# Four more weight remainders by accumulating DMA, modulations in a scratch of their own, squares added in pairs, and three changed orders of work

## The reference

```python
x = first_block(x, c, w_ada, ...)                      # 256 x 1024, fp32 throughout
# even layer, for x and for the context
sh, sc, gt = _modulation(c, e_w_mod[i], e_b_mod[i])    # silu(c) @ w_mod + b_mod
x_new = x + gt * _even_mix(_pre(x, e_norm[i], sh, sc), *args)
xc = xc + gt_c * _even_mix(_pre(xc, e_norm[i], sh_c, sc_c), *args)
# _even_mix: u = silu(layernorm(dwconv(a_val * sigmoid(a_glu))))
#            y_a = (u @ a_pw_w + a_pw_b) * silu(a_gate)
#            y_b = fourier_mix(b_val) * silu(b_gate);  concat(y_a, y_b) @ w_out
# odd layer: modulations of its own, rms norms of x and xc, ODD_IN projection, window attention
# _pre(x, g, shift, scale) = rmsnorm(x, g) * (1 + scale) + shift
```

## Time and profile before

| | |
|---|---|
| median of three runs | 747.08 us (745.29 to 749.2) |
| profiled execution | 744.48 us, span 742.7 us |
| PE busy | 725.7 us, 98% of the span |
| DVE busy | 640.5 us, 86% |
| ACT busy | 393.1 us, 53% |
| POOL busy | 8.3 us, 1% |
| chain of work that ended last | PE 79%, DVE 9%, DMA 5%, ACT 3%, issue 2% |
| mean granted TensorE clock | 0.994 of full speed |
| L940 (subtractions) | 82, 2288 ns each |
| L415 (casts) | 90, 1906 ns each |
| L905 (modulation halves) | 88 + 48, 1220 ns each |

### The profile page before, as it was taken

How to read it: one execution, slowest core, us unless ns; L and a number is a source line. 1 busy time by engine, 2 the same in 40 slices (tenths; PEclk the granted TensorE clock), 3 DMA queues, 4 the chain that set the end, 5 groups by cost and what they waited for, 6 DMA issues and landing times.

```text
span 742.7 us, 12665 instructions
## 1 busy us (share of the span) xinstructions
PE 725.7 (98%) x5202; PEld 665.2 (90%) x5202; DVE 640.5 (86%) x1082; ACT 393.1 (53%) x532; POOL 8.3 (1%) x18
## 2 busy tenths in 40 slices
PE   8899999999999999999999999999989999999996
PEld 4789989999989999999999998888768899999995
DVE  5777898897998899999988999999899979888653
ACT  4254366668356555554557555345462345555742
POOL 0000000000000000000000000000000000000000
PEclk9999999999999999999999999999999999999998
DMA  9989999866664676666656176877405642675101
GB/s 367 420 323 395 388 395 355 315 245 216 220 227 170 221 255 253 236 227 235 248 199 227 57 248 157 219 206 192 113 23 227 226 144 83 221 275 187 58 1 57
DMA packets 24875, 163.98 MB, mean 221 GB/s; under 512 B 2758, under 2 KB 4591, under 8 KB 5360
## 3 DMA queue, kind: packets, MB, share of 16 engines
q1 hardware_dynamic: 21404, 150.37, 54.2%
q0 software_dynamic: 1152, 8.39, 5.6%
q10 hardware_dynamic: 2262, 4.42, 1.8%
HBM read 153.71 MB, written 1.07 MB: 208 GB/s over the span
## 4 chain that ended last, share of the span: by engine, by line
PE 79%; DVE 9%; DMA 5%; ACT 3%; issue 2%; DVEq 0%; ACTq 0%; SPq 0%
PE psum L1607 67%; DVE w_lo L905 4%; DMA raw<-in_w 4%; PE psum L1698 3%; DVE w_lo L940 2%; DMA arena<-in_w 2%; ACT w_hi L415 1%; PE psum L2102 1%; PE psum L2126 1%; PE psum L2114 1%; PE psum L1789 1%; PE psum L1646 1%; PE psum L1771 1%; PE psum L1675 1%; DVE xs L1415 0%
## 5 line engine op out<-in xcount | busy, mean ns | idle before, releaser
L1607 PE MATMUL psum<-h_hi,w_hi 128*128 128x256 f32 (+1 forms) x1280 | 386.3, 302 | 3.5 <-DVE h_lo L1381 2.2
L1607 PE MATMUL psum<-h_lo,w_hi 128*128 128x256 f32 (+1 forms) x1280 | 382.6, 299 | 0.0
L1607 PE MATMUL psum<-h_hi,w_lo 128*128 128x256 f32 (+1 forms) x1280 | 382.5, 299 | 0.0
L1607 PEld LDWEIGHTS psum<-h_hi,w_hi 128*128 128x128 f32 x1280 | 244.6, 191 | 13.8 <-issue 4.1
L1607 PEld LDWEIGHTS psum<-h_lo,w_hi 128*128 128x128 f32 x1280 | 244.7, 191 | 7.9 <-issue 0.2
L1607 PEld LDWEIGHTS psum<-h_hi,w_lo 128*128 128x128 f32 x1280 | 244.6, 191 | 7.5
L940 DVE TENSOR_TENSOR w_lo<-raw,w_hi 128x2048 fp32r<-128x2048 f32 x82 | 187.6, 2288 | 26.1 <-ACT w_hi L415 25.2
L415 ACT CAST w_hi<-raw 128x2048 fp32r<-128x2048 f32 x90 | 171.3, 1906 | 38.9 <-DMA raw<-in_w 29.8
L905 DVE SCALAR_TENSOR_TENSOR w_lo<-raw,cond 128x1024 fp32r<-128x1024 f32 x88 | 104.2, 1220 | 0.8
L905 DVE SCALAR_TENSOR_TENSOR w_lo<-raw,arena 128x1024 fp32r<-128x1024 f32 x48 | 56.8, 1220 | 11.4 <-DMA raw<-in_w 5.8
L638 ACT ACTIVATE arena<-psum,vec 128x256 f32<-128x256 f32 x44 | 22.5, 564 | 58.6 <-DVE g_lo L1182 54.2
(11 more groups left out here) (246 smaller groups left out, 710.0 us busy)
## 6 DMA issues: line engine op xcount, KB each, us to landing
raw<-in_w SPq DMA_DIRECT2D x138, 1024.0 KB, 4.9
w_lo<-raw POOLq DMA_DIRECT2D x8, 1024.0 KB, 7.2
arena<-in_w SPq DMA_DIRECT2D x3, 1024.0 KB, 14.6
xs<-in_xs SPq DMA_DIRECT2D x1, 1024.0 KB, 9.0
consts<-diff ACTq DMA_DIRECT2D x4, 256.0 KB, 9.2
cond<-diff ACTq DMA_DIRECT2D x1, 1024.0 KB, 8.6
xs<-in_xs ACTq DMA_DIRECT2D x1, 1024.0 KB, 7.5
out<-xs SPq DMA_DIRECT2D x2, 384.0 KB, 2.5
```

The costliest lines, as they stand in the source:

```text
L1607: last = mm(out, w[a], x[b], start=start and n == 0, stop=stop and n == 2, skip_group_check=skip)
```

## The change

- `BY_DMA` takes in chunks 73 to 76 as well: twelve chunks instead of eight get their low half by negation on ACT and an adding DMA.
- The modulations 39 to 43 (`MODS_APART`) write their products into `arena[:, 8448:9472]` (free there) instead of a `w_lo` slot. They no longer wait for that slot; since all four products go to one place, each waits for the one before.
- In `split` on DVE the modulations before a chunk are done even where the chunk itself goes by DMA. m39 is done in one piece, behind the splits of the Fourier tiles.
- ACT's `load_ln_exp` stands behind the four squares instead of before them.
- Fourier tiles 2 and 3 are gated in the loop that scales and splits `u`, at `t` = 3 and 5.
- Squares of the main tokens' tiles 0 to 5 are added in pairs on DVE (`add_squares_of`), one pair after chunk 73's evacuation, one after chunk 74's, and one after the bias and the coefficients; PE sums three tiles instead of six and waits for all three pairs before. The semaphore of the context's pairs is shared (now 6).
- In `staggered` PE also waits for the remainder of the first chunk.
- On PE, at `h` = 1, `stick_scores(0)` comes before `transposed_probs(0)`.

```diff
-BY_DMA = tuple(range(LIN_EIN + 4, LIN_EIN + 12))
+BY_DMA = tuple(range(LIN_EIN + 4, LIN_OIN + 1))
+MODS_APART = range(39, 44)
@@ scalar, after the even input chunks
-            load_ln_exp()
             for t in range(4):
                 act.wait_ge(sem("centered"), t + 1)
                 nc.scalar.activation(ln_tmp[:, t, :], conv[:, t, :], ACT.Square).then_inc(sem("ln_squares"), 1)
                 if t < 2:
                     fourier_evac(t + 2)
+            load_ln_exp()
             act.wait_ge(sem("ln_sum"), 2)
@@ vector, mod
-                if not isinstance(j, int) or j >= SPL + AS_LOADED:
+                apart = m in MODS_APART
+                products = arena[:, 8448:8448 + D] if apart else None
+                if not apart and j >= SPL + AS_LOADED:
                     dve.wait_ge(sem("lin_done"), LIN_OPEN + j - (SPL - 1))
...
                     for t in range(2):
+                        if apart and (t or v):
+                            if t:
+                                me.mark(last)
+                            me.wait()
                         last = nc.vector.scalar_tensor_tensor(
-                            w_lo[:, slot, D * t:D * (t + 1)], raw[:, rslot, D * t:D * (t + 1)], 1.0, c, ALU.mult, ALU.mult,
+                            products if apart else w_lo[:, slot, D * t:D * (t + 1)], raw[:, rslot, D * t:D * (t + 1)], 1.0, c, ALU.mult, ALU.mult,
                             accum_out=modv[:, bass.ds(4 * m + 2 * t + v, 1)])
@@ vector, split
-                    if j in BY_DMA:
-                        return
                 if isinstance(j, int):
                     for mod_before in mods_before(j)[done:]:
                         mod_static(mod_before, j)
                     mod_before = (mods_before(j) or [None])[-1]
+                    if j in BY_DMA:
+                        return
@@ vector, even layer
-                if t == 1:
-                    fourier_gated(1)
+                if t in (1, 3, 5):
+                    fourier_gated((t + 1) // 2)
 
             (m,) = mods_before(LIN_EOUT + 1)
-            mod_static(m, LIN_EOUT + 1, part=0)
...
-                    if t >= 2:
-                        fourier_gated(t)
...
-            mod_static(m, LIN_EOUT + 1, part=1)
+            mod_static(m, LIN_EOUT + 1)
             split(LIN_PW + 2, done=1)
...
+            def add_squares_of(name, k):
+
+                tiles = gain_sq if name == "odd_ctx" else norm_tmp
+                dve.wait_ge(sem(f"sq_{name}"), k + 2)
+                nc.vector.tensor_tensor(tiles[:, k, :], tiles[:, k, :], tiles[:, k + 1, :], ALU.add).then_inc(sem("odd_added"), 1)
...
+                if i in (1, 2):
+                    add_squares_of("odd_x", 2 * i - 2)
                 if i == 2:
-                    split(LIN_OIN, done=2)
                     mod_bias(36, 44)
                     coefficients(32, "o_norm", mod_row(O_SC, 0))
                     coefficients(40, "o_norm", mod_row(O_SC, 1))
+                    add_squares_of("odd_x", 4)
@@ tensor, staggered
+                if j in BY_DMA:
+                    remainder_ready(j)
                 remainder_ready(j + 1)
@@ tensor, first block, odd h
-                    transposed_probs(p)
                     if p:
+                        transposed_probs(p)
                         weighted_values(p - 1, 1)
                     stick_scores(p)
+                    if p == 0:
+                        transposed_probs(p)
@@ tensor, even output, after the first half of chunk 75
-                        sum_squares("odd_x", range(6))
+                        pe.wait_ge(sem("odd_added"), 3)
+                        sum_squares("odd_x", (0, 2, 4))
                     if s == 1 and m == 0:
                         sum_squares("odd_x", (6, 7))
-                        pe.wait_ge(sem("odd_ctx_added"), 3)
+                        pe.wait_ge(sem("odd_added"), 6)
                         sum_squares("odd_ctx", (0, 2, 4))
```

More of the change, by code:

```diff
@@ L1440, in _ @@
             for k in (0, 2, 4):
-                dve.wait_ge(sem("sq_odd_ctx"), k + 2)
-                nc.vector.tensor_tensor(gain_sq[:, k, :], gain_sq[:, k, :], gain_sq[:, k + 1, :],
-                                        ALU.add).then_inc(sem("odd_ctx_added"), 1)
+                add_squares_of("odd_ctx", k)
             split(LIN_OIN + 1)
```

## The result

| | before | after |
|---|---|---|
| median | 745.16 us (20 runs) | 747.98 us (20 runs) |
| ratio, 95% interval | | 1.0028 (1.0017 to 1.0040), +2.1 us |
| profiled execution, span | 744.48, 742.7 us | 749.54, 747.4 us |
| mean granted clock over the runs | 0.996 (the runs of before in the experiments) | 0.992 |

The forecast was −1.1 us; the kernel became 2.1 us slower (1.3 to 3.0); this is by the ratio, which is estimated from all runs, while the two medians lie 2.8 us apart. It stays inside the 0.5% that counts as no change, and inside the range, but on the other side of zero.

A forecast was written before the change was run, and what follows sets the result against it. PE, busy 98% of the span, was taken as the bound, so only its breaks and removed PE work could be won. −0.77 − 0.35 = −1.1 us gave 743.4 profiled, median 746.0, range 743.0 to 749.0.

The forecast's parts named there:

- what covers the rest: Check that low halves of chunks 73 to 76 and the load for modulation 41 arrive in time; cost taken as 0.
- the added transfers come late: Rival: transfers take three times 7.2 us, PE stands 9.5 us for chunk 75; 755.5 us; chance 0.05.
- the clock falls in the new wait: Rival: PE's 2.8 us idle before the sums lowers the clock, costing 1.7 us of matmul; 747.7 us; chance 0.15.
- the forecast wait: PE's wait for the third addition of squares before its three sums, some 2.8 us, ending at 590.1 us.
- steps 2 to 4: Table load, Fourier tiles and modulation 39, and added DMAs with pairs: together 0.35 us won at the sums.
- step 1: Stick-breaking scores ahead of the first transposed probabilities on PE at h = 1; gain 0.77 us, bounds 0 and 1.1.
- the rival (0.18): Weight loads swallow the gain of the reordered scores at h = 1; only −0.35, 746.7 us; chance 0.18.
- Step 2: ACT's table load at 528.33 moved behind the squares; gain 0.49 us, bounds 0 and 0.5.
- Step 3: Fourier tiles 2 and 3 gated earlier, first half of modulation 39 later on DVE; gain 0.27 us, bounds 0 and 0.3.
- Step 4, DVE's walk: DVE followed from modulation 39 at 555.9 to the third addition's end at 590.05; PE goes on at 590.1.
- Step 4, pairs of squares: Squares added in pairs on DVE, 0.36 us each; three sums less save PE 1.3 us, but it waits for all additions.

The follow-up runs named there:

- experiment 9: Changed kernel with the adding transfer of chunk 74 cut to 16 of its 2048 columns; 746.54 us, 1.0002 to the kernel before.
- experiment 10: Changed kernel with the adding transfers of chunks 74 and 75 both cut to 16 columns; 747.03 us, 1.0009 to the kernel before.
- experiment 6: Changed kernel with 14 matmuls of zeros on PE ahead of its wait for chunk 75; 747.23 us, 1.0024 to the kernel before.
- experiment 12: Kernel of experiment 9 with 12 matmuls of zeros where PE waits for the third addition of squares; 745.56 us, 0.9995 to the kernel before.
- experiment 8: Kernel before with only the stick-breaking scores put ahead of the transposes at h = 1; 745.63 us, 0.9998.
- experiment 11: Kernel of experiment 5 with the old order of scores and transposes at h = 1; 743.00 us, 0.9961 to the kernel before.
- experiment 2: Kernel before with scores ahead, table load behind the squares and Fourier tiles gated earlier, modulation 39 not moved; 744.06 us, 0.9982.
- experiment 3: Changed kernel with the first half of modulation 39 back at its old place; 749.55 us, 1.0048 to the kernel before.
- experiment 5: Kernel of experiment 2 with chunk 73 alone added by DMA, modulation 39 apart at its old places, no main-token pairs; 743.45 us, 0.9970 to the kernel before.
- experiment 7: Changed kernel without the pairs of main-token squares, so PE sums six tiles; 748.27 us, 1.0040 to the kernel before.
- experiment 1: Changed kernel with the old order at h = 1, transposes before stick-breaking scores; 748.92 us, 1.0043 to the kernel before.
- experiment 4: Changed kernel with chunk 74 subtracted on DVE again instead of by DMA; 748.84 us, 1.0043 to the kernel before.

## Why the prediction was wrong

**The step that failed** is in "what covers the rest". It took the slowing of loads beside a transfer at 0 (bounds 0 to 2.5 us), on the grounds that DVE had 0.8 us to spare, and it followed only the load for modulation 41. Take 2.0 us off the times of the profile after, since PE was that much behind the forecast when it came to the last pointwise tile (555.65 against 554.42 − 0.76): then modulation 39 began at 555.9 and SP's load went out at 561.0, both as walked. The load took 9.7 us, just under the "twice" of the upper bound, and DVE waited 2.95 us. Two things were not carried on. The load of chunk 75 goes out 0.4 us behind it and is the third transfer beside the other two: 11.8 us where the walk had counted 4.9, so the negation ended at 577 instead of 572. And the transfer behind it, again beside loads, took 10.8 instead of 7.2. The low half stood ready at 588.1 instead of 579.2, for a need at 584.2: 5.0 us of cover were there and 8.9 were used up, 3.9 us too many; PE came 0.35 us later than walked and waited 3.6. All three signs that the prediction had named for being wrong came: DVE waited for the load before 41, a new transfer landed above 9 us, and the sums started without a wait. All of this was in reach before the run: the walk itself had a transfer and two loads of 1 MB each under way between 561 and 567, and took for each a duration from rows in which it ran alone. The Trainium skill ("DMA: Bandwidth & Descriptors", section "Rules for kernel authors") says of two transfers to disjoint partition halves that they use the same 16 engines and gain nothing over one; the trace agrees for a transfer and two loads: by the shares of the profile after (worked out in the last section) they need 5.2 + 2 × 2.8 = 10.8 us of all 16 engines, and from the first issue to the last landing 13.0 us passed (562.29 to 575.26), with a third load coming in at 568.3 and a fourth at 572.5.

**Rival "the added transfers come late"** had the right place and the right sign with 0.05. It was priced at three times the duration and argued away by the earlier trace rows. But those rows show transfers that run mostly alone. In the trace of before the transfers of the even input are issued at 496.9, 507.8 and 518.6 us, and the loads at 504.0 and 515.0, each just when the transfer ahead of it has landed (7.1 and 7.2 us), since SP waits for it; a load then overlaps the next transfer by 1 us. Where the overlap was longer, 3.5 us at 464.3, the transfer took 8.5. (The longest of those rows, 9.2 us at 453.4, had 0.8 us of a load beside it and stays unexplained.) In the stretch of the change SP has modulation chunks in its order, whose loads wait for DVE and not for the transfer, and so the two come together. The argument was about DVE and never asked what else was moving. DVE's work does not tell the short transfers from the long ones: in before, those at 496.9 and 518.6 us took 7.0 to 7.1 with DVE busy 6.9 of 7.0 us, and in the changed kernel DVE is busy 71% of the time under the transfer of 73 (7.0 us) and under that of 74 (10.2 us) alike; those of 74 to 76 took 10 us and more wherever loads ran beside them. The Trainium skill's rule ("SBUF — State Buffer", section "SBUF: two separate sides"), which the prediction set against the change, doesn't reach this case as the page has it: a DVE operation starves the descriptors while it runs in a 2-port mode, and one with two SBUF inputs, as a modulation or a subtraction is, gets in the way only of a GpSimd operation that reads SBUF. The trace agrees, with 7.0 us under such operations back to back. No run took DVE's modulations away, so a share of it in the longer ones is not excluded.

**Rival "the clock falls in the new wait"** (0.15) came true beside it: in the changed kernel behind the wait for chunk 75, and in experiments 9 and 10 behind the very wait that it named. It was priced well: 1.7 us of matmul at the lower level, against 2.4 us on the 24 short matmuls in the profile after. In the timed runs the mean granted clock fell from 0.996 to 0.992, which is 746 × 0.004 = 3 us of full-speed work not done. Not all of that shows in the time: over the 20 runs of the changed kernel the time rises by 0.56 us (standard error 0.13) for each such microsecond. That makes 1.7 us, an estimate from scatter, while experiments 6 and 12 kept the clock up in one place and won 0.3 and 0.5 by the middles, with overlapping intervals. The two parts can't be added neatly, since in experiment 6 the late addition took over where the clock had been.

**Sum by the runs.** The error is 3.2 us, from −1.1 to +2.1. The collision of the transfer of 74 with the loads is 1.9 of it (experiment 9: +2.1 to +0.15). Of the other 1.3 the clock behind the forecast wait is 0.5 by experiment 12 (+0.15 to −0.4); the last 0.7 is smaller than the intervals, which are 1 us to either side, and is left open.

**The same from marks in the traces.** PE has a 0.16 us wait for a square at 215.3 us and another at 735.5 (times of before), in every trace. Between these two lie 520.15 us in before, 524.35 in the changed kernel, 522.44 in experiment 9 and 519.62 in experiment 12, where the transfer of 74 is out and the clock up: −0.5 us, against −0.35 forecast for steps 2 to 4. So these steps were priced rightly but for the collision and the clock. The 2.8 us between experiments 9 and 12 are what a clock down for 6.8 us cost in one profiled execution; the timed runs of the two differ by 0.5 only, and their mean clocks by less than the two profiles' do. Ahead of the first mark the change has step 1 alone. PE reaches it between 213.9 and 216.2 us, on the average at 215.2 in the 11 traces with step 1 and at 215.7 in the three without, a difference smaller than the spread: the open 0.7 us may be step 1's.

**Step by step.**
- Step 1: right in the trace, its gain not shown. The bracket at the first transposes is gone (but for experiment 8, with its late load) and, in five of the traces, one of 0.2 to 0.4 us stands at the second; yet experiments 8 and 11 find no gain. They speak for the rival (0.18), by which the weight loads set the pace in this stretch, but within intervals that hold the forecast 0.77 too. DVE's normalisation began anywhere between 100.9 and 103.4 us in the traces, and PE's lead of 0.8 us is small against that.
- Step 2: right in the mechanism, and worth more than its upper bound. The table load stands at 532.67 behind the fourth square, none before the first, and PE has no idle time before the sum behind it. From the mark at 215.3 us to the first matmul behind the stop at 541, PE takes 325.35 us in the two traces without this step and 324.6 to 324.7 in the twelve with it: 0.7 us, where 0.49 was forecast and 0.5 was the bound. It is the most exact figure of the study; where the last 0.2 come from was not looked into.
- Step 3: right for both halves together. The wait for the last pointwise low half is 0.3 us instead of 0.56. Where the first half of modulation 39 kept its place (experiments 2, 3, 5 and 11) the wait was 0.7 to 0.8 instead: in experiment 2, which moves the Fourier tiles alone, the step loses a little.
- Step 4, DVE's walk: right where the loads were in time. In experiment 9 the third addition ran from 590.27 and PE went on at 590.75 (2.89 us of waiting); forecast 590.1, and 590.5 if the 0.44 us by which that trace was behind at the last pointwise tile are added.
- Step 4, pairs of squares: three sums less are won even here (experiment 7, +0.9 without them, with overlapping intervals).
- The range of 743 to 749 held the result; the chances of the slower side (0.05 for late transfers, 0.15 for the clock) were too small. The late load had been given no weight of its own, and a stop of 2.9 us, as the forecast itself contained, had the clock down behind it in both traces that have one.

## What to carry to other kernels

When work is moved from an engine to a DMA, write down all that the DMA engines carry in that stretch, in their order of issue, and follow each transfer to its user: the one that is late is not the one moved, but a load that goes out beside it, and a chain of load, cast, negation and transfer pays twice (here 6.9 us at the load and 3.6 at the transfer). Give a move to places where the DMA engines are idle (chunk 73, at 545 us, −0.9 us on top of steps 1 to 3 by the middles) and stop there. Several small waits gathered into one long one are not of equal value: both traces with a stop of 2.9 us in one piece had the clock down behind it, where 0.9 us had left it up.

## What the runs showed of the hardware

- An adding transfer of 1 MB from SBUF to SBUF took 7.0 to 7.3 us with at most 2.4 us of a load beside it (once 7.8 and once 9.2) and 10.0 to 14.4 us beside loads throughout; a 1 MB load took 4.7 to 5.0 us in before between 559 and 600 us and mostly 7.3 to 15.9 us beside such a transfer. Two loads issued 0.4 us apart, without one: 4.7 to 7.0 us (experiment 9). By the shares of the profile after, (8.4% × 747.4) / 12 = 5.2 us of all 16 engines go to one adding transfer and 53.8% × 747.4 us over 150.37 MB, 2.8 us for a MB, to a load. A low half by DMA costs the DMA engines nearly as much as two loads.
- The same 2.2 us stop of PE at 541 us let the clock fall, for 3.4 us, in the profiles of the changed kernel and of experiments 1, 4, 6 and 10, and left it up in that of the kernel before and of 2, 3, 5, 7, 8, 9, 11 and 12. What decides it the runs don't show. Where it fell, the fall cost 1.6 us (15.12 us to the last pointwise tile in the changed kernel, 13.56 in experiment 7). The stops of 3.5 to 4.0 us for chunk 75 or the addition (changed kernel, experiments 1, 4 and 7) and the two of 2.9 (9 and 10) all had the lower clock with them, for 3.4 to 6.9 us; so had the pair of 2.4 and 1.9 us in experiment 3, for 3.4. Stops of up to 1.8 us behind the head left it up in every trace.
- The weight loads of the first block vary: DVE's normalisation behind them began up to 2.4 us apart from trace to trace, in kernels that are the same up to there but for step 1.
